# Folding a final norm and the next block's first norm into one normalisation, with the residual rescaled during the following projection

## The reference, cut to what matters

```
y  = rmsnorm(h, final_norm)            # eps 1e-6, end of first_block
# second_block, i = 0
mod = silu(c) @ ada_w[0] + ada_b[0];  sh1, sc1, g1, ... = split(mod)
n  = rmsnorm(y, norm_mix_g[0])         # eps 1e-5
x1 = n * (1 + sc1) + sh1               # input of the S5 mixer
y  = y + g1 * s5_mixer(x1)             # the residual needs y itself
```

## Time and profile before

| what | value |
|---|---|
| median of three runs | 3088.75 us |
| span of the profiled execution, first to last instruction | 3086.1 us |
| PE / DVE / ACT / POOL busy | 94% / 52% / 34% / 39% |
| mean granted TensorE clock | 0.956 of full |

### The profile page before, as it was taken

The page is one execution under the profiler, slowest core; times in us unless marked ns, Lnnn a source line. Parts: engine busy times, 40 slices in busy tenths (PEclk is TensorE's granted clock), DMA queues, the critical chain, the costliest instruction groups (busy, mean ns, idle before and its releaser), DMA issues.

```text
span 3086.1 us, 38851 instructions
## 1 busy us (share of the span) xinstructions
PE 2914.6 (94%) x14565; PEld 2374.3 (77%) x14565; DVE 1617.9 (52%) x2275; ACT 1049.6 (34%) x1327; POOL 1212.1 (39%) x556
## 2 busy tenths in 40 slices
PE   7999999999999999999998799999999988999998
PEld 6867886788877856788886677788878776778887
DVE  4435554776868146564556635555354766232224
ACT  4341122434332245333333222222235554232222
POOL 3433422344444410344443114444434544534443
PEclk9998998999999999999998779999999998999999
DMA  4320001334532320355533733655322322223322
GB/s 137 95 72 14 1 1 28 109 115 129 152 111 94 109 69 28 123 177 164 191 120 119 234 88 128 213 191 164 97 82 85 115 89 69 69 87 100 99 96 68
DMA packets 343961, 326.44 MB, mean 106 GB/s; under 512 B 28816, under 2 KB 320144, under 8 KB 343696
## 3 DMA queue, kind: packets, MB, share of 16 engines
q1 hardware_dynamic: 309760, 257.34, 26.9%
q10 hardware_dynamic: 34064, 67.18, 6.2%
HBM read 303.44 MB, written 21.04 MB: 105 GB/s over the span
## 4 chain that ended last, share of the span: by engine, by line
PE 72%; DVE 7%; issue 3%; ACT 2%; DMA 0%; POOL 0%; ACTq 0%; DVEq 0%; SPq 0%; POOLq 0%
PE bank L248 18%; PE bank L250 18%; PE bank L249 18%; PE bank L260 3%; PE bank L265 3%; PE bank L261 3%; PE bank L1328 2%; DVE lw L2576 1%; PE bank L1346 1%; PE bank L1336 1%; PE bank L1901 1%; PE bank L1896 1%; PE bank L2622 1%; PE bank L361 0%; DVE xt L404 0%
## 5 line engine op out<-in xcount | busy, mean ns | idle before, releaser
L238 POOL TENSOR_TENSOR w_lo<-w_raw,w_hi 128x1024 fp32r<-128x1024 f32 x400 | 1006.9, 2539 | 1446.0 <-ACT w_hi L209 1430.4
L248 PE MATMUL bank<-x_hi,w_hi 128*128 128x512 f32 x2032 | 799.5, 393 | 12.8 <-POOL w_lo L238 7.5
L250 PE MATMUL bank<-x_hi,w_lo 128*128 128x512 f32 x2032 | 793.3, 390 | 0.0
L249 PE MATMUL bank<-x_lo,w_hi 128*128 128x512 f32 x2032 | 793.1, 390 | 0.0
L209 ACT ACTIVATE w_hi<-w_raw 128x2048 fp32r<-128x2048 f32 x208 | 398.0, 1914 | 893.5 <-PE bank L250 787.5
L248 PEld LDWEIGHTS bank<-x_hi,w_hi 128*128 128x128 f32 x2032 | 383.7, 189 | 96.7 <-issue 14.9
L249 PEld LDWEIGHTS bank<-x_lo,w_hi 128*128 128x128 f32 x2032 | 383.5, 189 | 80.7 <-issue 1.6
L250 PEld LDWEIGHTS bank<-x_hi,w_lo 128*128 128x128 f32 x2032 | 382.9, 188 | 80.3
L248 PE MATMUL bank<-m_hi,w_hi 128*128 128x512 f32 x384 | 149.6, 390 | 0.0
L250 PE MATMUL bank<-m_hi,w_lo 128*128 128x512 f32 x384 | 149.4, 389 | 0.0
L249 PE MATMUL bank<-m_lo,w_hi 128*128 128x512 f32 x384 | 149.4, 389 | 0.0
(11 more groups left out here) (437 smaller groups left out, 4762.1 us busy)
## 6 DMA issues: line engine op xcount, KB each, us to landing
w_raw<-in_mlp_w SPq DMA_DIRECT2D x128, 512.0 KB, 4.5
ada_w<-in_ada_w ACTq DMA_DIRECT2D x96, 512.0 KB, 4.9
w_raw<-in_f_w_up SPq DMA_DIRECT2D x88, 512.0 KB, 5.1
w_raw<-in_m_w_in SPq DMA_DIRECT2D x40, 512.0 KB, 4.7
w_raw<-in_a_w_in SPq DMA_DIRECT2D x32, 512.0 KB, 4.7
w_raw<-in_f_w_down SPq DMA_DIRECT2D x32, 512.0 KB, 4.0
w_raw<-in_w_kv SPq DMA_DIRECT2D x16, 512.0 KB, 4.3
w_raw<-in_s_w_glu SPq DMA_DIRECT2D x16, 512.0 KB, 5.3
```

The source lines that it names most:

```text
L238: op = pool.tensor_tensor(w_lo[s][:, part], w_raw[s][:, part], w_hi[s][:, part].bitcast(F32), ALU.subtract)
L248: pe.matmul(dst, hi_l, hi_r, start=start, stop=False)
L249: pe.matmul(dst, hi_l, lo_r, start=False, stop=False)
L250: return pe.matmul(dst, lo_l, hi_r, start=False, stop=stop)
```

## The change

- Norms 4 and 5 become one (the later ones are renumbered). The squares in the last down projection are weighted: mid_c = final_norm² + 1e-5, by a scalar_tensor_tensor in place of a tensor_tensor; the root's bias is 1e-11, and the gain of the mixer's norm is multiplied by final_norm in ada_mod_dve.
- The unweighted squares of h are formed by ACT (mid_squares_act, tiles 0 to 5 in the last down projection's loop, 6 and 7 at the head of s5_act) and added up by DVE in a buffer of their own (mid_start_dve, mid_add_dve: two additions ahead of each of the last three slots' add_h, two at the head of s5_dve).
- PE sums them between the two halves of S5's slot 1, ACT takes the root ahead of s_u_act(0), DVE the reciprocal, PE spreads it into bank 6 after slot 1, and DVE rescales the 8 tiles of h (mid_scale_dve) ahead of S5's own work. mid_dve and mid_act go.
- A semaphore is saved (cond_in becomes silu_done), a memset and two small weights operations are added early in the program.

```diff
-            slot_body(pe, base + 1, rhs_hi, rhs_lo, kt, (1,))(0)
+            if between is None:
+                slot_body(pe, base + 1, rhs_hi, rhs_lo, kt, (1,))(0)
+            else:
+                pe_slot_start(pe, base + 1)
+                slot_half(pe, 1, 0, rhs_hi, rhs_lo, kt)
+                between()
+                slot_half(pe, 1, 1, rhs_hi, rhs_lo, kt)
...
-            dve.tensor_tensor(sqs[0][:, o, :], hk, hk, ALU.mult).then_inc(n_sq, 1)
+            if weight is None:
+                dve.tensor_tensor(sqs[0][:, o, :], hk, hk, ALU.mult).then_inc(n_sq, 1)
+            else:
+                dve.scalar_tensor_tensor(sqs[0][:, o, :], hk, weight(k), hk, ALU.mult, ALU.mult).then_inc(n_sq, 1)
...
+                        if c == 2 and i < 3:
+                            mid_squares_act(act, 2 * i, 2)
...
                 if c == 2:
                     squares_start(dve, c_norm, SQ_X)
+                    if f:
+                        mid_start_dve(dve)
                 for i in (0, 2):
                     for s in range(2):
                         ada(c, 1, i + s)
-                        add_h(dve, base_dn, i + s, s, c_norm if c == 2 else None, SQ_X)
+                        if f and c == 2 and i + s:
+                            mid_add_dve(dve, 2 * (i + s) - 2, 2)
+                        add_h(dve, base_dn, i + s, s, c_norm if c == 2 else None, SQ_X, (lambda k: mid_c[:, k:k + 1]) if f else None)
                         if f and c == 2 and i + s == 2:
                             ada_mod_dve(dve, 0)
...
+            if f == 0:
+                dve.wait_ge(mod_done, 2)
+                dve.tensor_tensor(gain[:, 0, 0:8], gain[:, 0, 0:8], par[:, PAR["final_norm"]:PAR["final_norm"] + KD],
+                                  ALU.mult).then_inc(mod_done, 1)
...
-        def mid_dve(dve, c, c_next):
-            norm_root(dve, c)
-            squares_start(dve, c_next, SQ_B)
+        def mid_start_dve(dve):
+
+            dve.wait_ge(mid_acc, 2)
+            dve.memset(mid_sum[:, :], 0.0).then_inc(mid_acc, 1)
+
+        def mid_squares_act(act, first, count):
+
+            for k in range(first, first + count):
+                act.wait_ge(bank_free, 2 * SLOTS["f1_dn2"] + k + 1)
+                act.wait_ge(mid_acc, 2 + max(k, 1))
+                act.activation(sq[:, k % 2, :], h[:, k, :], ACT.Square).then_inc(mid_sq, 1)
+
+        def mid_add_dve(dve, first, count):
+
+            for k in range(first, first + count):
+                dve.wait_ge(mid_sq, k + 1)
+                dve.wait_ge(mid_acc, k + 3)
+                dve.tensor_tensor(mid_sum[:, :], mid_sum[:, :], sq[:, k % 2, :], ALU.add).then_inc(mid_acc, 1)
+
+        def mid_sums_pe(pe):
+
+            pe.wait_ge(mid_acc, KD + 3)
+            for j in range(TT):
+                mm = pe.matmul(bank[4][:, j:j + 1], mid_sum[:, j * P:j * P + P], ones[:, 0:1], start=(j == 0), stop=(j == TT - 1))
+            mm.then_inc(mid_done, 1)
+
+        def mid_root_act(act):
+
+            act.wait_ge(mid_done, 1)
+            act.activation(ncol[:, 0, :], bank[4][:, 0:TT], ACT.Sqrt, bias=eps_col[:, 0:1], scale=1.0 / D).then_inc(mid_done, 1)
...
+        def mid_scale_dve(dve):
+
+            dve.wait_ge(mid_done, 4)
             for k in range(KD):
-                dve.scalar_tensor_tensor(h[:, k, :], h[:, k, :], pcol("final_norm", k), RSTD, ALU.mult, ALU.mult).then_inc(mid_done, 1)
-                if k:
-                    add_square(dve, c_next, k - 1, (k - 1) % 2, SQ_B)
-
-        def mid_act(act, c_next):
-
-            for k in range(KD):
-                act.wait_ge(mid_done, k + 1)
-                act.wait_ge(n_acc, k + squared(c_next))
-                act.activation(sq[:, k % 2, :], h[:, k, :], ACT.Square).then_inc(n_sq, 1)
-
+                dve.scalar_tensor_tensor(h[:, k, :], h[:, k, :], pcol("final_norm", k), MID_BANK[:, :], ALU.mult,
+                                         ALU.mult).then_inc(mid_done, 1)
...
-            first_turn(pe, base, x_hi, x_lo, normed(lots), ready_hi=normed_hi(lots))
+            first_turn(pe, base, x_hi, x_lo, normed(lots), ready_hi=normed_hi(lots), between=lambda: mid_sums_pe(pe))
+            mid_spread_pe(pe)
...
+            mid_squares_act(act, 6, 2)
+            mid_root_act(act)
             s_u_act(act, 0)
...
+            mid_add_dve(dve, 6, 2)
+            mid_rcp_dve(dve)
+            mid_scale_dve(dve)
             dve.wait_ge(gemm_ready, 2 * SLOTS["s_in"] + 1)
...
-            norm_act(act, 4, 0, split=False)
-            mid_act(act, 5)
-            norm_act(act, 5, 1, 5, shift=lambda k: mod[:, 0, k:k + 1], slot=SLOTS["s_in"])
+            norm_act(act, 4, 2, 5, shift=lambda k: mod[:, 0, k:k + 1], slot=SLOTS["s_in"])
...
-            mid_dve(dve, 4, 5)
-            norm_dve(dve, 5, 5, lambda k: gainc(0, k), shift=lambda k: mod[:, 0, k:k + 1], slot=SLOTS["s_in"])
+            norm_dve(dve, 4, 5, lambda k: gainc(0, k), shift=lambda k: mod[:, 0, k:k + 1], slot=SLOTS["s_in"])
```

More of the change, by code:

```diff
@@ L131, in build @@
         ncol = sb("ncol", [P, 3, TT])
-        eps_col = sb("eps_col", [P, 2])
+        eps_col = sb("eps_col", [P, 3])
+        mid_c = sb("mid_c", [P, KD])
         nar_hi = sb("nar_hi", [P, KD, 32], F32R)
@@ L250, in three, with first_turn @@
             return pe.matmul(dst, lo_l, hi_r, start=False, stop=stop)
-        def first_turn(pe, base, rhs_hi, rhs_lo, ready, kt=KD, ready_hi=None):
+        def first_turn(pe, base, rhs_hi, rhs_lo, ready, kt=KD, ready_hi=None, between=None):
             pe_slot_start(pe, base)
@@ L324, in squares_start, with square @@
             dve.memset(sqs[1][:, :], 0.0).then_inc(n_acc, 1)
-        def square(dve, c, k, o, sqs, sem_h, value):
+        def square(dve, c, k, o, sqs, sem_h, value, weight=None):
             dve.wait_ge(sem_h, value)
@@ L407, in norm_dve, with add_h @@
             low(KD - 1)
-        def add_h(dve, base, i, s, c, sqs):
+        def add_h(dve, base, i, s, c, sqs, weight=None):
             for o in range(2):
@@ L416, in add_h @@
                 if c is not None:
-                    square(dve, c, i * 2 + o, o, sqs, bank_free, n)
+                    square(dve, c, i * 2 + o, o, sqs, bank_free, n, weight)
         x_tok = at("x_tok", 40, [P, TT, D])
@@ L450, in load_act @@
         def load_act(act):
-            act.wait_ge(ones_set, 4)
+            act.wait_ge(ones_set, 5)
             act.wait_ge(x_in, 16)
@@ L469, in load_dve @@
             dve.memset(eps_col[:, 1:2], EPS2).then_inc(ones_set, 1)
+            dve.memset(eps_col[:, 2:3], EPS1 * EPS2).then_inc(ones_set, 1)
             dve.memset(nar_raw[:, :, 16:32], 0.0).then_inc(ones_set, 1)
@@ L1134, in ffn_act @@
             if f == 0:
-                act.activation(cond[:, :], par[:, PAR["cond"]:PAR["cond"] + 8], ACT.Silu).then_inc(cond_in, 1)
+                act.activation(cond[:, :], par[:, PAR["cond"]:PAR["cond"] + 8], ACT.Silu).then_inc(silu_done, 1)
             for c in range(3):
@@ L1195, in ffn_dve @@
             if f:
-                dve.wait_ge(cond_in, 1)
+                dve.wait_ge(silu_done, 25)
             for c in range(3):
@@ L1446, in mid_act @@
-        def mid_act(act, c_next):
-            for k in range(KD):
-                act.wait_ge(mid_done, k + 1)
-                act.wait_ge(n_acc, k + squared(c_next))
-                act.activation(sq[:, k % 2, :], h[:, k, :], ACT.Square).then_inc(n_sq, 1)
+        mid_done, mid_sq, mid_acc = sem("mid_done"), sem("mid_sq"), sem("mid_acc")
+        mid_sum = at("mid_sum", 80, [P, T])
+        MID_BANK = bank[6]
+        def mid_start_dve(dve):
+            dve.wait_ge(mid_acc, 2)
+            dve.memset(mid_sum[:, :], 0.0).then_inc(mid_acc, 1)
@@ new lines, in mid_sums_pe, with mid_rcp_dve @@
+        def mid_sums_pe(pe):
[6 more added lines that the diff above has]
+            act.activation(ncol[:, 0, :], bank[4][:, 0:TT], ACT.Sqrt, bias=eps_col[:, 0:1], scale=1.0 / D).then_inc(mid_done, 1)
+        def mid_rcp_dve(dve):
+            dve.wait_ge(mid_done, 2)
+            dve.reciprocal(ncol[:, 0, :], ncol[:, 0, :]).then_inc(mid_done, 1)
@@ new lines, in mid_spread_pe @@
+        def mid_spread_pe(pe):
+            pe.wait_ge(mid_done, 3)
+            for j in range(TT):
+                mm = pe.matmul(MID_BANK[:, j * P:j * P + P], ncol[:, 0, j:j + 1].to_broadcast([P, P]), ident[:, :],
+                               start=True, stop=True)
+            mm.then_inc(mid_done, 1)
+        def mid_scale_dve(dve):
+            dve.wait_ge(mid_done, 4)
+            for k in range(KD):
+                dve.scalar_tensor_tensor(h[:, k, :], h[:, k, :], pcol("final_norm", k), MID_BANK[:, :], ALU.mult,
+                                         ALU.mult).then_inc(mid_done, 1)
@@ L1525, in s_par_act, with mid_weight_dve @@
             act.activation(sc(CO), sc(T1), ACT.Sin).then_inc(s_act, 1)
+        def mid_weight_dve(dve):
+            g = par[:, PAR["final_norm"]:PAR["final_norm"] + KD]
```

(43 more changed lines are left out.)

4 lines of the change are left out of this document (1 added, 3 removed).

## The result

The changed kernel takes **3141.28 us** (median of 5 runs, 3140.5 to 3142.15) against 3090.31 us for the kernel before in the same session (5 runs, 3088.41 to 3091.66): ratio 1.0165, 95% interval 1.0153 to 1.0177. It is 51 us slower, where 4 us less were forecast.

A forecast was written before the change was run, and what follows sets the result against it. PE, busy 94% of 3086.1 us, was taken as the bound, with a serial seam between blocks. The terms -16.29 + 6.7 + 4.85 + 0.75 = -4.0 us gave 3084.7 us from 3088.75, range 3077.3 to 3090.3.

The forecast's parts named there:

- Everything else in the sum is measured against that: At the seam of the blocks: other terms count against the first scaled tile starting at 1654.00 in place of 1670.29.
- After the first state product the order of PE, DVE and loads is as now: Behind the seam, from the first state product on: order unchanged, so no further term in the sum.
- Removed, -16.29: Seam from 1654.00 to 1670.29: the second norm's serial chain goes, 16.29 us less.
- DVE in the last down projection: Added DVE work and waits for POOL end the last square at 1655.9; first scaled tile 6.7 us later, bounds 0 and 12.
- rival B: Last down projection: seventh running sum starts before POOL, only the last square waits; 2.8 us less, 3081.9 us; chance 0.27.
- Last square to first scaled tile: At the merged norm: 4.8 us from the end of the last square to the first scaled tile.
- ACT behind the root: S5's slot 1: evacuations and split queue behind the root; slot 2 starts 4.85 us later, bounds 2.0 and 6.8.
- Clock: PE's new wait of 2.9 us before slot 2 may cost the full clock: 0.75 us, bounds 0 and 1.5.
- some 3 us: After PE's wait before slot 2: matmuls at half speed if the clock falls, 1.5 us lost, half of it taken.
- The rescale: Eight DVE operations on h, 5.4 us, hidden in DVE's idle time before its first rotation.
- D: Last down projection: more DVE operations caught by POOL, 2.0 us each; three more give 3090.7 us; chance 0.09.
- A case "slower": Whole kernel slower by over 0.2%, above 3094.9 us, as a tail of D; chance 0.05.

The follow-up runs named there:

- e6: The changed kernel with mid_c in free room at the arena's end, nothing else moved: 3085.04 us, ratio 0.9982 to the kernel before.
- e5: The kernel before with 32 unused bytes ahead of w_hi only, so weights and arena both move by 32 bytes: 3091.08 us, ratio 1.0004.
- e15: The kernel before with triu (512 bytes) allocated ahead of w_hi, arena unmoved: 3091.24 us, ratio 0.9999.
- e12: The changed kernel with mid_c allocated ahead of w_raw, so all large buffers move by 32 bytes together: 3085.39 us, ratio 0.9983.
- e7: e6 with the second root behind the split of slot 2's weights in ACT's queue: 3079.49 us, ratio 0.9965 to the kernel before.
- e8: e7 with the additions of tiles 4 and 5 also moved to the head of s5_dve: 3079.40 us, ratio 0.9961 to the kernel before.
- e18: The kernel before with gain, cond, ncol and eps_col (256 bytes together) ahead of w_hi, arena unmoved: 3089.07 us, ratio 0.9997.
- e1: The kernel before with an unused buffer of 32 bytes ahead of the arena: 3144.15 us, ratio 1.0171.
- e4: The kernel before with 32 unused bytes ahead of w_hi and 32 more ahead of the arena: 3144.71 us, ratio 1.0171.
- e2: The changed kernel with an unused pad of 32 bytes, arena 64 bytes from its old place: 3103.31 us, ratio 1.0038 to the kernel before.
- e3: The kernel before with 64 unused bytes ahead of the arena: 3106.84 us, ratio 1.0056.
- e10: The kernel before with 96 unused bytes ahead of the arena: 3145.06 us, ratio 1.0176.
- e13: The kernel before with gain (128 bytes) allocated ahead of w_hi, arena unmoved: 3139.21 us, ratio 1.0158.
- e19: The kernel before with mod (384 bytes) allocated ahead of w_hi, arena unmoved: 3139.76 us, ratio 1.0159.
- e14: The kernel before with cond and eps_col (64 bytes together) allocated ahead of w_hi, arena unmoved: 3145.02 us, ratio 1.0171.
- e9: The kernel before with eps_col (32 bytes) allocated ahead of w_hi, arena unmoved: 3141.53 us, ratio 1.0174.

## Why the prediction was wrong

**The step that failed** is the sentence that the sum was made of the seam alone: "Everything else in the sum is measured against that", and behind it "After the first state product the order of PE, DVE and loads is as now". The order is as before, and PE has eight matmuls fewer and less idle time. Their pace isn't, and no step asked where the new buffers go and what they push. The allocation of mid_c has no term in the sum and no rival. Put in (after less e6), it is 3141.28 - 3085.04 = +56.2 us. The profile shows it as PE's busy time, 2979.8 us against e6's 2921.2. The difference of 58.6 us at 0.2333 - 0.2267 us each is, as an estimate, some 8,800 of PE's 14,557 matmuls. No row of the trace before could price this, but the diff showed two edited lines ahead of `arena = nc.sbuf_base`.

**The seam** is read in e6, where nothing else moved. Times are counted from POOL's first stretch in the last down projection (1622.16 before, 1625.11 in e6). e6's profiled execution took 3091.24 us, the longest of its eleven, so its span of 3089.4 us doesn't show the gain. The seam repeats far better than the whole: from POOL's first stretch to the first state product it takes 78.89 us before, 78.80 in e5 and 78.83 in e15, whose seams are as before, and 73.90 in e6 and 73.85 in e12. The chain of waits of e6, start, length, what:
```profile
1653.61 0.69 DVE h L425
1654.33 2.13 DVE sq_x L341
1656.50 1.88 PE bank L364 x8
1658.94 2.09 PE bank L371 x8
1661.05 0.76 DVE xt L414
...
1681.78 0.80 PE bank L1483 x8
1682.86 0.50 ACT ust L2016
1683.76 0.61 ACT ust L2016
1684.82 1.93 ACT w_hi L210
1686.97 2.29 issue
1689.26 2.37 POOL w_lo L239
1691.68 0.68 PE bank L249
1699.01 2.02 PE bank L1943 x64
```
- *Removed, -16.29.* As forecast. One norm stands where two stood: square, sums, spread, first scaled tile, and nothing between.
- *DVE in the last down projection: +6.7 forecast, +4.1 measured.* The first scaled tile comes 1661.05 - 1625.11 = 35.94 us into it; the norm's factors were there at 1654.00 - 1622.16 = 31.84 us before. This is rival B: DVE and POOL in e6, start, length, engine, line:
```profile
1644.93 2.77 DVE L350 TENSOR_TENSOR sq_x_sum<-sq_x_sum,sq_x 128x512 f32<-128x512 f32 x1
...
1647.98 2.00 DVE L1258 SCALAR_TENSOR_TENSOR gain<-mod,par 128x8 f32<-128x8 f32 x1
...
1653.00 0.69 DVE L350 TENSOR_TENSOR sq_x_sum<-sq_x_sum,sq_x 128x512 f32<-128x512 f32 x1
1653.61 0.68 DVE L425 TENSOR_TENSOR h<-bank,h 128x512 f32<-128x512 f32 x1
1654.33 2.12 DVE L341 SCALAR_TENSOR_TENSOR sq_x<-h,mid_c 128x512 f32<-128x512 f32 x1
```
```profile
1653.01 5.64 POOL L239 TENSOR_TENSOR w_lo<-w_raw,w_hi 128x1024 fp32r<-128x1024 f32 x2 [3.06 <-ACT w_hi L210]
```
  The seventh tile's running sum starts at 1653.00, 0.01 us ahead of POOL, and takes 0.69 us. Only the last square waits out a half. In the changed kernel as given it starts 0.52 us ahead (1675.19 against POOL's 1675.71) and isn't caught either. The forecast used the rule of the Trainium skill, SBUF — State Buffer, Who interferes with whom (whichever issues first gets the pair), to say that POOL wins here. Both traces agree with the rule: the operation that started first ran its 0.69 us, the one that started behind POOL took 2.12. My starting times were 0.1 us off, on a margin of 0.1.
- *Last square to first scaled tile: 4.8 forecast;* 1661.05 - 1656.45 = 4.6 measured.
- *ACT behind the root: +4.85 forecast, +4.6 measured.* Slot 1 starts at 1676.17 and slot 2 at 1691.68, 15.5 us on (15.8 forecast, 10.9 before), released by POOL after a wait of 2.62 us (2.9 forecast):
```profile
1676.17 0.39 PE L249 MATMUL bank<-x_hi,w_hi 128*128 128x512 f32 x1
...
1691.68 0.68 PE L249 MATMUL bank<-x_hi,w_hi 128*128 128x512 f32 x1 [2.62 <-POOL w_lo L239]
```
  e7 takes this wait away and gains 5.5 us in the median.
- *Clock: +0.75 forecast, +2.6 measured.* The wait did cost the full clock (in e7, without the wait, slot 1's end and slot 2 run at 1.00), and there was a second place that the sum didn't have, slot 0 itself. Windows of e6:
```profile
1662.00:1668.00 6.00, 5.24 (x13) 4.18 (x14) 5.67 (x9) 3.40 (x5) 0.00 (x0) 0.50 0.75 240
1668.00:1674.00 6.00, 6.00 (x28) 4.96 (x27) 5.69 (x9) 3.22 (x5) 0.00 (x0) 1.00 0.00 0
...
1693.00:1696.00 3.00, 3.00 (x10) 2.37 (x9) 1.57 (x6) 0.00 (x0) 3.00 (x2) 0.62 1.04 292
```
  Slot 2 runs at half clock until about 1695.3: from its start to the state product it takes 7.33 us against 1701.05 - 1695.45 = 5.6 before, +1.7. The forecast's "some 3 us" at half speed named no row; here it is 3.6 us, and the fall came, where the forecast took half of its price. Slot 0, from first scaled tile to end, takes 15.1 us against 14.3, +0.8: it runs at half clock until 1668.1, 5.3 us behind its first matmul, and before only until about 1675.6, 3.6 us behind it, as the window that opens with slot 0 before shows:
```profile
1672.00:1678.00 6.00, 6.00 (x20) 4.82 (x21) 5.86 (x9) 2.84 (x5) 0.00 (x0) 0.72 0.00 0
```
- *The sum:* -16.29 + 4.1 + 4.6 + 2.6 = -5.0 at the first state product; the medians say -4.95, e12's -4.0. That the forecast's -4.0 for the seam comes so near is partly luck: 2.6 us too much for DVE and 1.9 too little for the clock cancel. The rescale took 5.36 us, and behind it DVE still waited 5.61 us for the first rotation in the changed kernel as given: hidden, as forecast. No table load stood on the path.

Of the rivals B held in its place, but its time was out of reach. D didn't happen. A case "slower" got 0.05, and its mechanism was a seam that runs late; the loss came from outside the seam.

## What to carry to other kernels

An edit that allocates has a cost of its own: write down which buffers move, and keep the distance between the stationary and the moving operands of the main matmuls as it was (small new buffers ahead of everything, as in e12, or at the end, as in e6). When a time comes out far from the sum, first compare how many matmuls start in a window that PE fills at full clock; here 443 against 430 set the waits aside at once. Then judge the edit in a version with nothing moved: this one is worth -0.18%, and with the root behind the split (e7) -0.35%, 3079.5 us.

## What the runs showed of the hardware

The pace of back-to-back matmuls of 128x512 at full clock, both operands of the type float32r, depends on the distance in bytes a partition from the stationary operand's buffer (w_hi, w_lo) to the moving one's (x_hi and so on). As far as tried it repeats every 256:

| distance, over a multiple of 256 | runs | matmuls in 2820 to 2920 us | ratio |
|---|---|---|---|
| 0 | before, e5 to e8, e12, e15 to e18 | 442 to 443 | 0.998 to 1.000; e7 0.9965, e8 0.9961 |
| 32 | changed kernel, e1, e4 | 430, 430, 431 | 1.0165 to 1.0171 |
| 64 | e2, e3 | 439 | 1.0038, 1.0056 |
| 96 | e10 | 431 | 1.0176 |
| 128 | e13, e19 | 430, 432 | 1.0158, 1.0159 |
| 192 | e14 | 431 | 1.0171 |
| 224 | e9 | 430 | 1.0174 |

The slow cases cost up to 3% of each such matmul (0.2333 us from start to start in place of 0.2267; at 64 it is 0.2289) and 1.6 to 1.8% of the kernel. A few matmuls have the roles the other way round, w_hi moving and x_hi stationary, 256 columns. They did not slow down, before and e1:
```profile
L248 PE MATMUL bank<-w_hi,x_hi 128*128 128x256 f32 x128 | 36.2, 283 | 0.0
```
```profile
L249 PE MATMUL bank<-w_hi,x_hi 128*128 128x256 f32 x128 | 36.0, 281 | 0.0
```
So the table holds for the shape and the roles that it names, and other shapes weren't measured for it. Why a remainder of 64 costs so little (0.4 to 0.6%), what 160 does, and which part of the chip is behind it stay open; w_hi to w_lo and x_hi to x_lo kept their distances in every run, so the two weight buffers, or the two moving ones, weren't told apart.
